# Two extra landing places for the next expert's first two weight units, filled ahead and copied by GpSimd into the ring in quarters; the slot weights spread by bf16 matmuls

## What is computed

```python
logits = (xt @ p['w_router']).astype(F32) + p['b_router']
topv, topi = lax.top_k(logits, TOP_K)          # 4 of 32 experts
wts = jax.nn.softmax(topv, axis=-1)
# for each block of tokens of one expert e:
gu = xb @ p['w_gu'][e] + p['b_gu'][e]          # 1024 -> 2048
gate = jnp.minimum(gu[:, :D_FF], SWIGLU_LIMIT)
up = jnp.clip(gu[:, D_FF:], -SWIGLU_LIMIT, SWIGLU_LIMIT)
act = (up + 1.0) * gate * jax.nn.sigmoid(SWIGLU_ALPHA * gate)
out[tok] += (act @ p['w_down'][e] + p['b_down'][e]) * w[:, None]   # 1024 -> 1024
```

## Time and profile before

| what | value |
|---|---|
| median of three runs | 1636.38 us |
| lowest, highest | 1625.16, 1641.66 us |
| the profiled execution's own time | 1639.18 us |
| its span, first to last instruction | 1637.2 us |
| mean granted TensorE clock, of full speed | 0.918 |
| PE busy, of the span | 1409.4 us (86%) |
| DVE busy | 593.5 us (36%) |
| ACT busy | 271.5 us (17%) |
| POOL busy | 59.9 us (4%) |
| bytes moved, mean rate | 505.67 MB, 309 GB/s |

### The profile page before, as it was taken

The page is one execution under the profiler, slowest core; times in us unless marked ns, Lnnn a source line. Parts: engine busy times, 40 slices in busy tenths (PEclk is TensorE's granted clock), DMA queues, the critical chain, the costliest instruction groups (busy, mean ns, idle before and its releaser), DMA issues.

```text
span 1637.2 us, 40360 instructions
## 1 busy us (share of the span) xinstructions
PE 1409.4 (86%) x16383; PEld 786.5 (48%) x16384; DVE 593.5 (36%) x1314; ACT 271.5 (17%) x635; POOL 59.9 (4%) x111
## 2 busy tenths in 40 slices
PE   5998989999999689979999797887859897789794
PEld 2445656367676345535555353443425443344452
DVE  2334656344623423323333232422413322132324
ACT  2024532211110311101111010110101111011111
POOL 2021310000000000000000000000000000000000
PEclk8999989988999699979999898988979998898897
DMA  9644992940291289599999999999999969996940
GB/s 356 244 138 149 354 395 70 375 141 1 56 340 68 103 360 400 237 423 384 383 402 396 423 400 422 411 401 423 409 428 419 405 261 421 425 427 258 414 201 32
DMA packets 71439, 505.67 MB, mean 309 GB/s; under 512 B 6528, under 2 KB 6648, under 8 KB 35332
## 3 DMA queue, kind: packets, MB, share of 16 engines
q1 hardware_dynamic: 63588, 480.98, 72.6%
q0 software_dynamic: 7808, 24.12, 4.5%
HBM read 499.97 MB, written 5.11 MB: 308 GB/s over the span
## 4 chain that ended last, share of the span: by engine, by line
PE 64%; DMA 24%; DVE 6%; issue 2%; SPq 1%; ACT 1%; POOL 0%; DVEq 0%; ACTq 0%; POOLq 0%
PE psum L517 58%; DMA ring<-in_w_gu 15%; DMA ring<-in_w_down 7%; DMA ring<-in_w_ada 2%; PE psum L681 1%; PE psum L1016 1%; PE psum L971 1%; DVE region L1282 1%; PE psum L993 1%; SPq L2198 1%; DVE region L1131 0%; PE psum L713 0%; ACT region L1765 0%; DVE region L1249 0%; SPq L2203 0%
## 5 line engine op out<-in xcount | busy, mean ns | idle before, releaser
L517 PE MATMUL psum<-ring,region 128*32 128x256 f32 (+1 forms) x11072 | 663.1, 390 | 126.2 <-DMA ring<-in_w_gu 123.7
L517 PEld LDWEIGHTS psum<-ring,region 128*32 128x32 f32 x11072 | 345.6, 113 | 394.2 <-DMA ring<-in_w_gu 135.2
L1678 DVE TENSOR_TENSOR region<-region,psum 128x1280 f32<-128x1280 f32 x110 | 163.3, 1485 | 554.2 <-PE psum L517 554.2
L1765 ACT ACTIVATE region<-psum 128x256 f32<-128x256 f32 (+6 forms) x385 | 160.7, 420 | 1136.7 <-PE psum L517 495.3
L517 PE MATMUL psum<-region 32*128 32x320 f32 (+10 forms) x2652 | 245.6, 421 | 9.1 <-ACT region L1765 3.4
L517 PEld LDWEIGHTS psum<-region 128*32 128x32 f32 (+5 forms) x2652 | 105.6, 139 | 110.3 <-issue 73.9
L517 PE MATMUL psum<-hT,ring 128*128 128x320 f32 x448 | 124.9, 437 | 0.0
L517 PEld LDWEIGHTS psum<-hT,ring 128*128 128x128 f32 x448 | 84.7, 192 | 35.6 <-issue 2.5
L517 PE MATMUL psum<-ring,hT 128*128 128x512 f32 (+1 forms) x192 | 86.6, 608 | 1.9 <-ACT hT L1788 1.9
L1656 DVE TENSOR_SCALAR region<-region 128x128 f32<-128x128 f32 x165 | 47.3, 344 | 110.0 <-issue 110.0
L517 PEld LDWEIGHTS psum<-ring,hT 128*128 128x128 f32 (+1 forms) x192 | 33.2, 177 | 51.1 <-issue 50.0
(11 more groups left out here) (300 smaller groups left out, 852.8 us busy)
## 6 DMA issues: line engine op xcount, KB each, us to landing
ring<-in_w_gu SPq DMA_DIRECT2D x128, 2048.0 KB, 11.7
ring<-in_w_down SPq DMA_DIRECT2D x64, 2048.0 KB, 10.9
ring<-in_w_ada SPq DMA_DIRECT2D x12, 2048.0 KB, 14.2
ring<-in_w_in SPq DMA_DIRECT2D x11, 2048.0 KB, 19.7
ring<-in_cache_k SPq DMA_DIRECT2D x64, 256.0 KB, 5.3
ring<-in_cache_v POOLq DMA_DIRECT2D x64, 256.0 KB, 5.4
ring<-in_w_out SPq DMA_DIRECT2D x2, 2048.0 KB, 23.2
ring<-in_w_up_a SPq DMA_DIRECT2D x1, 2048.0 KB, 16.7
```

What stands on the lines that cost most here:

```text
L517: return pe.matmul(out, lhsT, rhs, start=start, stop=stop, skip_group_check=True)
L1678: dve.tensor_tensor(acc_pairs[:, r], acc_pairs[:, r], psum[:, B_SUM:B_SUM + GROUPS, 0:NT], ALU.add)\
L1765: return act.activation(out, src, ACT.Copy)
```

## The change

- **Two landings.** `landing[0]` and `landing[1]`, 2 MB each, are carved from SBUF that is free by then. SyncE no longer loads units 0 and 1 of experts 1 to 31 into the ring. `fill_landing(i, e)` loads unit i of expert e into `landing[i]`. That of expert 1 is issued for unit 0 after the normed tokens were transposed, for unit 1 after the plan is complete. In the loop SyncE issues units 2, 3, 4, 5 of expert e and then the landings of units 0 and 1 of expert e+1; the landing waits for the four copies out of it (`piece_moved[i]`).
- **GpSimd copies.** For each expert GpSimd waits for the landing and for the last read of the ring place, and copies the 4096 words per partition in four pieces of 1024, unit 0 first, then unit 1. Each piece increments `piece_moved[i]`. TensorE's quarters 0 and 1 wait for each piece, ahead of the four matmuls (eight in the profile's count) that read it.
- **Slot weights.** `turn_weights`, the three `selw` operations of VectorE and the copy by ScalarE go. Places and weights are kept by expert as three bf16 rows per value that sum to it (`place_weight`, 96 x 640, made once). Per block VectorE copies a one-hot column (`weight_hot`, 96x128 bf16), TensorE spreads places and weights with two bf16 matmuls of 320 columns (`spread_weights`, after `down`), and VectorE compares and multiplies (two operations of 128x320) straight into `selwT`.
- **Registers.** TensorE loads the next expert's number in the middle of the block rather than both numbers at its start.

The core of the diff:

```diff
@@ TensorE
             def gate_up_quarter(c, expert):
 
-                pe.wait_ge(unit_landed[moe_slot[c]], 16 * expert + (landed_base[c] + 16))
+                if c >= LANDINGS:
+                    pe.wait_ge(unit_landed[moe_slot[c]], 16 * expert + (landed_base[c] + 16))
                 u = ring[:, moe_slot[c], :].rearrange("p (j f) -> p j f", j=2)
                 for j in range(2):
                     for q, out_bank in ((0, B_GATE), (1, B_UP)):
+                        if c < LANDINGS:
+                            pe.wait_ge(piece_moved[c], PIECES * expert + (2 * j + q + 1))
                         last = spread(out_bank, hgT[:, j, LANES[c]],
...
-            def turn_weights():
-                for j, (t0, m) in enumerate(TILES):
-                    last = pe.transpose(psum[:, B_Y, t0:t0 + m], selw[0:m, j, :], ident[0:m, 0:m])
-                last.then_inc(selw_turned, 1)
+            def spread_weights():
+
+                for i in range(2):
+                    last = mm(psum[:, B_SUM + i, 0:NT], weight_hot, place_weight[:, NT * i:NT * i + NT], True, True)
+                last.then_inc(weights_spread, 1)
...
                 if not first:
                     pe.wait_ge(actT_copied, b)
                     down(before_expert)
+                    pe.wait_ge(weight_hot_ready, b)
+                    spread_weights()
...
+                    next_expert = load_next()
                     pe.wait_ge(y_copied, b)
+                    pe.wait_ge(selw_ready, b)
                     combine(0)
...
                     combine(1)
-                pe.wait_ge(selw_ready, b + 1)
-                turn_weights()
+                    pe.reg_mov(expert_last, expert)
+                    pe.reg_mov(expert_now, next_expert)
@@ the plan, TensorE and VectorE
             for j, (t0, n) in enumerate(TILES):
-                last = pe.transpose(out[0:NE, t0:t0 + n], wts[0:n, j, :], ident[0:n, 0:n])
+                for g in range(3):
+                    last = mm(out[NE * g:NE * g + NE, t0:t0 + n], wts[0:n, j, :], ident[0:n, 0:n], True, True)
...
+            out = claim(pe, ALLB, "placeT")
+            for j, (t0, n) in enumerate(TILES):
+                for g in range(3):
+                    last = mm(out[NE * g:NE * g + NE, t0:t0 + n], eq[0:n, j, :], ident[0:n, 0:n], True, True)
...
+            for rows in (3 * NE, 2 * NE, NE):
+                step(dve.tensor_copy(place_weight[0:rows, :], split_f32[0:rows, :]))
+                if rows > NE:
+                    rest = split_f32[0:rows - NE, :]
+                    step(dve.tensor_tensor(rest, rest, place_weight[0:rows - NE, :], ALU.subtract))
@@ VectorE, per block
-            def slot_weights(column, expert):
-                for j in range(3):
-                    last = dve.tensor_scalar(selw[:, j, :], lanes, pos[:, j, column], wts[:, j, expert],
-                                             ALU.is_equal, ALU.mult)
-                last.then_inc(selw_ready, 1)
+            def hot_weights(expert):
+
+                dve.tensor_copy(weight_hot, const("expert_hot", 3 * NE)[:, expert].to_broadcast([3 * NE, P]))\
+                    .then_inc(weight_hot_ready, 1)
+
+            def slot_weights(b, round_):
+
+                dve.wait_ge(weights_spread, b + 1)
+                dve.tensor_scalar(selwT, psum[:, B_SUM, 0:NT], place[:, round_], None, ALU.is_equal)\
+                    .then_inc(slot_found, 1)
+                dve.wait_ge(slot_found, b + 1)
+                dve.tensor_tensor(selwT, selwT, psum[:, B_SUM + 1, 0:NT], ALU.mult).then_inc(selw_ready, 1)
@@ GpSimd
+            with pool.Fori(1, NE) as e:
+                before = pool.value_load(ints[0:1, bass.ds(e + (AT_BLOCKS - 1), 1)], min_val=1,
+                                         max_val=MAX_BLOCKS)
+                filled = nc.snap(16 * e, [mybir.EngineType.Pool])
+                for i in range(LANDINGS):
+                    pool.wait_ge(unit_landed[moe_slot[i]], landed_base[i] + 16)
+                    pool.wait_ge(unit_read[i], before)
+                    pool.wait_ge(landing_filled[i], filled)
+                    for piece in range(PIECES):
+                        part = slice(UNIT // PIECES * piece, UNIT // PIECES * (piece + 1))
+                        pool.tensor_copy(ring[:, moe_slot[i], part], landing[i][:, part])\
+                            .then_inc(piece_moved[i], 1)
@@ SyncE
+            def fill_landing(i, expert):
+
+                sp.dma_start(landing[i], gu[expert, i].rearrange("o p f -> p (o f)")).then_inc(landing_filled[i], 16)
...
             expert_weights(slice(0, 1), None)
+            sp.wait_ge(*full("h2", 2, 1))
+            fill_landing(0, slice(1, 2))
             sp.wait_ge(tables, 1)
-            with sp.Fori(1, NE) as e:
+            for m in range(KT):
+                sp.wait_ge(*drained("bd", m))
+            sp.wait_ge(weight_rows_ready, 1)
+            fill_landing(1, slice(1, 2))
+            with sp.Fori(1, NE - 1) as e:
...
                 expert_weights(bass.ds(e, 1), before)
+                for i in range(LANDINGS):
+                    sp.wait_ge(piece_moved[i], PIECES * e + PIECES)
+                    fill_landing(i, bass.ds(e + 1, 1))
```

More of the change, by code:

```diff
@@ L47 @@
 RING = 6
+LANDINGS = 2
+PIECES = 4
 REGION = 18120
@@ L62 @@
 AT_LATER = AT_BLOCKS + NE
-N_INTS = AT_LATER + 1
+AT_ROUND = AT_LATER + 1
+N_INTS = AT_ROUND + N_LIST
 def const_pack():
@@ L260, in build @@
         sel = E.take(3, SLOTS)
-        selw = E.take(3, P)
         selwT = E.take(NT)
+        pos = E.take(3, ROUNDS * NE)
         E.at = max(E.at, fin_at + KT * NT + 2 * FF)
         late_const = E.take(n_const - n_late)
+        wts = E.take(3, NE)
+        fin_ss = E.take(6)
+        fin_rstd = E.take(3)
+        plan_row = E.take(N_LIST)
+        fin_gain = E.take(D)
+        landing = [region[:, REGION + KT * NT - UNIT:REGION + KT * NT], Area(E.at).take(UNIT)]
         logits = E.take(3, NE)
         mask = E.take(3, NE)
-        wts = E.take(3, NE)
         eq = E.take(3, NE)
         part_logits = E.take(NT)
+        split_rows = Area(E.at).take(2 * NT)
         hot4 = E.take(3, TOPK, NE)
@@ L301, in build @@
         M0 = small[0:H, 20:29]
+        pool_word = small[0:1, 40:48]
         BG = small[0:H, 29:30]
@@ L369, in build @@
         bias_in = sem("bias_in")
+        weight_rows_ready = sem("weight_rows_ready")
+        landing_filled = [sem(f"landing_filled{i}") for i in range(LANDINGS)]
+        piece_moved = [sem(f"piece_moved{i}") for i in range(LANDINGS)]
         tables = sem("tables")
@@ L1075, in _ @@
             down(NE - 1)
+            pe.wait_ge(weight_hot_ready, blocks)
+            spread_weights()
             pe.wait_ge(y_copied, blocks)
+            pe.wait_ge(selw_ready, blocks)
             pe.wait_ge(hgT_copied, blocks + 1)
@@ L1679, in add_sums, with expert_block @@
                     .then_inc(added, 1)
-            def expert_block(b, column, expert, next_column, next_expert, first):
-                if not first:
-                    dve.wait_ge(selw_turned, b)
-                slot_weights(column, expert)
+            def expert_block(b, next_column, next_expert, last_expert, last_round, first):
                 dve.wait_ge(gathered, b + 1)
@@ L2045, in expert_block @@
                 act.activation(act_s, act_g, ACT.Sigmoid, scale=ALPHA).then_inc(gate_sig, 1)
-                act.wait_ge(selw_turned, b + 1)
-                if not first:
-                    act.wait_ge(combined, 2 * b)
-                copy(selwT, psum[:, B_Y, 0:NT]).then_inc(selwT_copied, 1)
             copy_gathered(0, True)
```

85 lines of the change are left out of this document (56 added, 29 removed).

## The result

The changed kernel takes **1656.55 us** in the median of 4 runs (1655.53 to 1657.84), the kernel before 1639.02 us on the same chip (4 runs, 1625.16 to 1646.4): a ratio of 1.011, 95% interval 1.0078 to 1.0142. It is slower by just over 1%. The profiled executions have spans of 1656.2 and 1637.2 us; the 19.0 us between them are what is explained here.

A forecast was written before the change was run, and what follows sets the result against it. TensorE bounds two-block experts, weight transfers one-block ones. From the median of 1636.4 us, -3.5 (landings) + 30 (copies) - 18.5 (block) + 2 (collisions) + 2.5 (plan) + 0.5 (end) = +13: 1649 us, range 1628 to 1692.

The forecast's parts named there:

- Part 1: Landings: nothing gained in the experts' loop, since transfer order is unchanged; expert 1's first wait at the start saved, -3.5 us.
- Part 2: GpSimd copies at 1.0 us a piece lengthen the loop behind one-block experts from 28.4 to 30.9 us: +30 us.
- the twelve: Intervals behind the twelve one-block experts, bound by the weights, 28.4 us in the mean; forecast 2.5 us longer each.
- Part 3: TensorE's block falls from 15.93 to 15.5 us; 42 blocks outside the twelve intervals save 0.44 us each: -18.5 us.
- just under: Two-block experts: the copies' loop of 30.9 us lies just under TensorE's 31.0 us, so it costs nothing there.
- Part 4: VectorE, ScalarE and GpSimd per block: mostly hidden, slack of 2.1 us at block end; +2 us (0 to 15).
- a sign that it was wrong: TensorE's bias rows or `turn_act` starting to wait on VectorE would show the forecast wrong; no size given.
- Part 5: Before and after the loop: more small matmuls in the plan, +2.5 us (0 to 4); last block's slot weights, +0.5 us.
- the faster one: Rival: landings shrink the waits behind one-block experts, 1550 us, or 1610 if only three experts gain; chance 0.09.
- the slow copies: Rival: from 1.2 us a piece the two units' copies queue in one- and two-block experts, 1.675 ms and up; chance 0.17.
- the port as the main cause: Rival: GpSimd and VectorE hold each other up at block boundaries, 13 us over nineteen experts, 1662 us; chance 0.15.
- the quick copies: Rival: at 0.65 to 0.8 us a piece the shorter block pays for the loop, 1630 to 1642 us; chance 0.14.

The follow-up runs named there:

- experiment 1: The change without landings and GpSimd copies, so the slot weights and register load alone: 1638.78 us, 0.9964 to 1.0004 of the kernel before.
- experiment 2: The kernel before with only the landings and GpSimd copies added, its slot weights kept: 1651.99 us, 1.003 to 1.0072 of the kernel before.
- experiment 3: The change without GpSimd's copies; TensorE waits for the landing alone and reads the ring's old weights: 1635.04 us, 0.9923 to 0.997 of the kernel before.
- 7: The change with `down` ahead of quarter 1 and `turn_act` between the halves of quarter 0: 1638.93 us, 0.9963 to 1.0016 of the kernel before.
- 9: The change with a landing for unit 0 only, unit 1 loaded straight into the ring: 1633.7 us, 0.9953 to 0.9992 of the kernel before.
- 8: The change without landings and copies, with `down` ahead of quarter 1 and `turn_act` early: 1658.39 us, 1.0045 to 1.0156 of the kernel before.
- experiment 6: The change with one copy of 4096 columns per unit instead of four of 1024: 1711.99 us, 1.0382 to 1.0503 of the kernel before.
- experiment 5: The change with each piece copied onto itself in the landing, TensorE waiting for the landing alone: 1638.66 us, 0.9956 to 1.0021 of the kernel before.
- experiment 4: The change with each GpSimd piece copying 512 instead of 1024 columns: 1641.95 us, 0.9965 to 1.0011 of the kernel before.

## Why the prediction was right

The forecast was 1649 us, slower by +13 of span; measured were +19.0 and 1656.55 us, inside its own range. In part it was luck, since errors in both directions met in the sum, and experiments 1 and 2, which take its two halves apart, missed their forecasts by 14 us one way and 10 the other. By its steps:

- **Part 1, the landings gain nothing in the loop:** right, by experiment 3. The start's gain of 3.5 us came as 2.1. In experiment 2 it is 3.3. In the change TensorE loses part of it again: its quarter 0, here at 587.17, takes 3.45 us at a granted clock of 0.53, and 1.91 us in experiment 2. The wait of 1.76 us on VectorE ahead of it falls into expert 0's block, and is most of what that block has more than before:

```profile
586.95 0.40 PE L535 MATMUL psum<-oT,bias_hot 96*32 96x256 bf16 x8 [1.76 <-DVE bias_hot L1708]
587.17 3.45 PE L535 MATMUL psum<-ring,region 128*32 128x256 f32 x32
```

```profile
585.50 1.01 DVE L1708 CAST bias_hot<-keep 96x32 bf16 x1
...
603.57 0.17 DVE L1708 CAST bias_hot<-keep 96x32 bf16 x1
```

  The cast took 1.01 us beside the copies of expert 1's units, and 0.17 us without them.
- **Part 2, a piece of 1.0 us and a loop of 30.9:** right. The pieces come each 0.98 us, the loop is 30.80 in the mean, +28.4 us for the twelve against +30. That the copies are the cause is shown from both sides: taken away (experiment 3) or taken out of the loop (7, 9), the time comes back. One detail is different from the working. With no copy in it, the loop does not fall below some 28.4 to 29 us, so "loop = sum of its steps" holds only while the copies are in it; this is one reason why experiments 1 and 3 gained less than I expected. The agreement of the twelve is also better than the working deserves. It took the loop from one row pair of 27.9 us, in which quarter 1 ran at full clock, and compared its 30.9 us with the mean of 28.4. That mean has four intervals in which quarter 1 and `down` ran at half clock for some 4 us, and 5.5 to 6.0 us, not 3.9, went by from its start to the next issue. The change has none, which saves 0.6 us an interval. The prediction didn't name that.
- **Part 3, the block:** the sum's term was too large. The block went from 15.93 to 15.56 us, 0.37 instead of 0.44, and 40 blocks gave 40 x 0.38 = 15.2 us. From these went 5.3 us in blocks away from the stalls that took more than 15.56, and 0.7 us in those right behind one. The net is -9.2, where parts 3 and 4 had -18.5 and +2. These 7.3 us are the largest error of the sum; the others are +1.4 (start), -1.6 (the twelve), -1.6 (before the loop) and +0.6 (expert 0's block). The 40 blocks are 8.3 us above 15.56 each (before, 2.3 above 15.94). Of these 8.3 us, 4.5 are waits on VectorE, under part 4. Most of the rest lies in first blocks of experts, as here at expert 9:

```profile
854.84 0.40 PE L535 MATMUL psum<-oT,bias_hot 96*32 96x256 bf16 x8
...
859.35 4.09 PE L535 MATMUL psum<-ring,region 128*32 128x256 f32 x72 [0.34 <-POOL ring L2211]
...
871.12 0.40 PE L535 MATMUL psum<-oT,bias_hot 96*32 96x256 bf16 x8
```

  This block took 16.28 us. Its quarter 1 meets the copies of unit 1 still under way: two blocks need 31.1 us of TensorE and the loop 30.8, so the slack that the working called "just under" is used up now and then. In experiments 1 and 9 the same excess is 0.2 and under 1 us.
- **Part 4, VectorE beside GpSimd:** the contention is there, and it holds TensorE up at a place that the prediction didn't price. Beside the copies in a two-block expert, and one block later without them:

```profile
791.79 0.89 DVE L1755 TENSOR_TENSOR region<-region 128x256 f32<-128x256 f32 x1 [0.29 <-ACT region L2102]
792.78 1.07 DVE L1758 SCALAR_TENSOR_TENSOR region<-region 128x256 f32<-128x256 f32 x1
...
807.50 0.42 DVE L1755 TENSOR_TENSOR region<-region 128x256 f32<-128x256 f32 x1 [0.29 <-ACT region L2102]
808.03 0.42 DVE L1758 SCALAR_TENSOR_TENSOR region<-region 128x256 f32<-128x256 f32 x1
```

  1.1 us more in the pair is hidden, as the prediction had it for these two: `turn_act` follows at 793.96 without a wait, and the bias rows stand 15.66 us apart. What isn't hidden is the small cast ahead of them, `bias_hot`, for which the next block's bias rows wait:

```profile
PE psum L535 <- DVE bias_hot L1708: 6.3, 8, 1.8
```

```profile
887.50 0.40 PE L535 MATMUL psum<-oT,bias_hot 96*32 96x256 bf16 x8 [0.89 <-DVE bias_hot L1708]
```

```profile
886.17 0.99 DVE L1708 CAST bias_hot<-keep 96x32 bf16 x1
```

  The block ahead of these bias rows took 16.38 us. There are eight such waits, 1.8 us at the start and 4.5 us in the 40 blocks, five of them at the end of blocks right behind an interval (16.1 us each). The kernel before has one, of 0.8 us. The prediction named bias rows that wait on VectorE as a sign that it was wrong; the sign came, and by its size it is 5.5 us of waits more than before, against the +2 (0 to 15) of the sum. The Trainium skill, "SBUF — State Buffer", Who interferes with whom, has the two engines share one port pair and a VectorE operation with two inputs in SBUF contend for it; the trace agrees (0.42 against 0.89 and 1.07 us).
- **Part 5:** the plan cost 2.4 us, as put, and not the 0.9 of the table. From the small matmuls that begin it to block 0 it was 14.7 us before and is 17.1 in the change (15.8 in experiments 1, 5, 8 and 9, with the same plan):

```profile
560.32 0.48 PE L517 MATMUL psum<-keep,region 128*32 128x1 f32 x6
```

```profile
558.75 1.75 PE L535 MATMUL psum<-keep,region 128*32 128x1 f32 x24
```

  It began 1.6 us earlier, which looks like chance: this kernel begins it at 558.8 us and that of experiment 6, all but the same up to there, at 561.9. The end cost 0.4 us, as put. A further 0.6 us went into expert 0's block (above).
- **The rivals:** the faster one falls with experiment 3, the slow copies with 0.98 us a piece, the port as the main cause with experiment 5, and the quick copies with 0.98 us a piece too.

**What stays open:** how far the transfers alone set the loop without copies, 28.4 to 29 us. They are without a gap in the intervals (DMA share 1.01 at 428 GB/s), and six units at that rate are 29.4 us, which is near, not equal. The landings of experiment 1 show them back to back in nine intervals of twelve; but no run changed the size of the transfers. Nor does a run tell why the two halves of the change don't add up in the intervals, or why quarter 1 and `down` ran at half clock for some 4 us in 4 of 12 intervals of the kernel before and of experiment 4, and in none of the change.

## What to carry to other kernels

Before adding places to a ring, look for the transfer at the head of the queue and for what releases it: places further back gain nothing while their transfers stand behind that one in order. A copy on the way from landing to ring costs little as long as it lies beside the next transfer; that of the last unit that a release depends on is paid. So if there is a landing at all, give it to the first unit alone (here 1633.7 against 1656.6 us); that even this one is worth having over none wasn't shown here. And when one loop comes within 1% of another, as the copies' 30.9 us and TensorE's 31.0, price some of both.

## What the runs showed of the hardware that was not expected

- GpSimd copies float32 within SBUF at 0.9 to 1.1 ns a column: 0.57 us for 512 columns, 0.98 for 1024, 3.60 for 4096.
- VectorE operations beside these copies lose less than one piece, not the row of four: `SCALAR_TENSOR_TENSOR` of 256 columns went from 425 to 603 ns in the mean, and from 0.42 to 1.07 us in the rows above, 0.65 us against a piece of 0.98. With one copy of 3.6 us the wait for a cast of 32 columns reached 3.5 us, against 1.8 with pieces, so splitting a GpSimd copy bounds what it does to VectorE.
- After a wait of some 10 us TensorE's first quarter has a granted clock of 0.50 to 0.59, most of it at 1.2 GHz: 3.2 to 3.6 us for the 1.93 of full speed, where no piece paces it. Whether quarter 1 and `down` do so too for long differs between intervals of one run. Before, they took 5.4 us at a granted clock of 1.00 in eight, and 7.0 to 7.6 us at 0.71 to 0.76 in four, 6.0 in the mean. In the change, paced by the pieces, they took 7.04 us each time, at 0.91 to 1.00.
